# An inference step with 32 experts on one core: decode rows given eight places of their own in every expert tile, the prompt routed before the last cache pages, expert rows written straight to their tokens

## The chip, the core and the metric

The kernel runs on one core of one Trainium2 chip. The metric is device time in microseconds (us) of one execution, the median of several. Lower is better.

## What is computed

One layer of a decoder for 1024 prompt rows and 8 decode rows, width 1024, all in fp32:

```python
hn = rmsnorm(x, ln1_g);  q, k, v, u = split(hn @ w_in)
attn = diff_attend(rope(q), rope(k), v)       # prompt: causal, 1024 rows
                                              # decode: 64 cache pages of K and V per row
s5   = s5_mix(u, state)                       # diagonal state space group, GLU
x = x + concat(attn, s5) @ w_out
t = rmsnorm(x, ln2_g)
g = argmax(t @ w_rg + b_rg);  e1, e2 = top_2(t @ w_re[g] + b_re[g])   # 4 groups of 8 experts
x = x + sum_c wts[c] * ((silu(t @ w_gate[e_c]) * (t @ w_up[e_c])) @ w_down[e_c])
y = rmsnorm(x, ln_f_g)
```

The decode rows read the paged cache: 8 x 64 pages, each 256 KB of K and 256 KB of V.

## The kernel before, in words

**One list for TensorE.** `make_plan` (L170) is a list scheduler: from `streams` (L77), which gives each unit of work a cost and what it comes after, it makes one order in which TensorE does the units, and the other engines walk the same list. A page unit `("K", ...)` or `("V", ...)` covers eight pages. When it is placed is set by three numbers, `PAGE_US` (the time of a unit's transfer), `PAGE_LAG` (from the release of a place to its transfer) and `PACE` (the least distance of two page units). Engines run in order: a unit whose input is late holds up all behind it. `banks` deals six PSUM banks out to the units in the same order.

**Pages.** SyncE loads eight pages at a time (L476) into one half of `ring`, two halves in turn; the transfer into a half is issued when TensorE has used the half's last eight (`s_pgfree`). There are 128 page units in four passes of 32: K and V for decode rows 0 to 3, then K and V for rows 4 to 7. Between a K pass and its V pass stand `m1`, `m2`, `m3` and `pt`, the softmax over all scores; a V unit needs its result. After each row's V pages come `ov` (L1165) and, after the last, `dout` and `dout2` (L1173 to L1184): the norm of the decode attention, with a root on GpSimd (`root`, L538).

**Around the pages.** The prompt's projections, attention heads (`S`, `C`, `T`, `O`), the S5 group (`bA` to `bG`) and the output projection (`out`, unit halves of four 128x512 matmuls) fill TensorE between page units. Each row tile then passes `hn`, `hs`, `hT`, `r`: second norm, store to `h2_scratch` (L650), eight transposes (L1967), router logits. The decode rows are tile 8 (`NT`) of the same chain.

**Routing.** `choose` and `route` are appended after the whole plan. For all nine tiles at once VectorE picks group and experts (L1468 to L1516), TensorE ranks the choices within each expert (`rank`, matmuls of 320 columns and less), VectorE works out tile and place of each choice (L1526 to L1571), and TensorE makes the list of row numbers (`ids`). Each expert has a tile of 128 places; an expert with more rows gets another, out of at most 16 extra tiles. `s_route` then releases all engines.

**Experts.** A loop over tiles, four in each turn. GpSimd gathers a tile's rows from `h2_scratch` (L662, indirect), TensorE turns them (`turn`, L2014), VectorE scales (`scale`, L1608), then gate and up product (8 matmuls), tanh on ScalarE (L912), silu on VectorE (L1615, L1617), `turn_he` (L2028), the down product. ScalarE copies the result out (L923) and stores the tile's 128 rows in one direct transfer to `y_scratch` (L925). SyncE loads 3 MB of weights for each tile (L492, L493) into four places.

**The end.** When all is stored (`s_stored`), GpSimd gathers the two expert rows of every token (L685, 18 indirect transfers), VectorE adds them with their weights (L1640) and scales (L1653). A tile that may not have been written must read as zero or finite: GpSimd therefore writes 16 tiles of zeros to `y_scratch` during the u projection (L564).

## Time and profile before

| | us |
|---|---|
| median of 3 runs | 1621.96 (1618.86 to 1623.68) |
| profiled execution | 1610.36 |
| its span, first to last instruction | 1608.2 |
| TensorE busy | 1311.4 (82%) |
| VectorE busy | 515.3 (32%) |
| ScalarE busy | 250.8 (16%) |
| GpSimd busy | 203.2 (13%) |
| mean granted TensorE clock | 0.905 |
| moved by DMA | 467.51 MB, mean 291 GB/s |

The profiled execution is 11.6 us (0.7%) faster than the median of the others; its own outside part is 1610.36 - 1608.2 = 2.2 us. Busy shares are means over stages of different kinds. In the rows below a time is from the span's start, "PE" is TensorE, "PEld" its weight loads, "DVE" VectorE, "ACT" ScalarE, "POOL" GpSimd, "SPq" and "ACTq" the queues of SyncE and ScalarE. TensorE's rows count two instructions for each fp32 matmul of the program.

### The profile page before, as it was taken

How to read it: one execution, taken by the hardware profiler on the slowest of the kernel's cores; microseconds unless marked ns; L12 is line 12 of the kernel's file. 1: busy time of each engine (PE TensorE's matmuls, PEld its weight loads, DVE VectorE, ACT ScalarE, POOL GpSimd, SP SyncE). 2: the span in 40 equal slices, each digit the busy share in tenths (PEclk: the TensorE clock that was granted, in tenths of full speed). 3: DMA queues.
4: the chain of work that ended last, by engine and by line, in shares of the span. 5: the costliest groups of instructions: out<-in, count | busy, mean ns of one | idle time of the engine just before them, and what ended most of it. 6: DMA issues, size and time to landing. Idle time of an engine off the chain costs nothing.

```text
span 1608.2 us, 22029 instructions
## 1 busy us (share of the span) xinstructions
PE 1311.4 (82%) x6908; PEld 640.2 (40%) x6908; DVE 515.3 (32%) x1331; ACT 250.8 (16%) x472; POOL 203.2 (13%) x329
## 2 busy tenths in 40 slices
PE   4887998999879687688977698997359999999960
PEld 2333454443334234344543233444324444444420
DVE  1440343433243454344553011122501111111118
ACT  2100111121002222222342000000001111111112
POOL 1110304040310200000000100010011011010015
PEclk9898999998779799899987799998569999999985
DMA  9599999868878989899948999934239999999937
GB/s 360 205 351 348 315 326 310 294 182 311 252 236 296 313 302 321 291 337 329 347 166 286 379 336 318 320 99 161 107 144 334 369 366 369 367 371 366 365 114 271
DMA packets 187745, 467.51 MB, mean 291 GB/s; under 512 B 23177, under 2 KB 23561, under 8 KB 179090
## 3 DMA queue, kind: packets, MB, share of 16 engines
q1 hardware_dynamic: 163602, 386.02, 68.1%
q0 software_dynamic: 19456, 63.66, 11.1%
q10 hardware_dynamic: 4608, 16.78, 2.5%
q8 instruction: 50, 0.82, 0.2%
q14 instruction: 29, 0.24, 0.0%
HBM read 422.97 MB, written 42.22 MB: 289 GB/s over the span
## 4 chain that ended last, share of the span: by engine, by line
PE 60%; DMA 16%; SPq 9%; DVE 7%; issue 5%; DVEq 2%; ACT 1%; POOL 0%; ACTq 0%; POOLq 0%; PEldq 0%
PE WA L1671 42%; PE SC L1671 10%; DMA ring<-in_cacheV 8%; SPq L476 7%; DMA ring<-in_cacheK 7%; PE OD L1671 4%; PE WA L2014 2%; SPq L465 1%; DVE st L1084 1%; DVE arena L1640 1%; PE WA L1772 1%; DMA xm<-in_xT 1%; DVE arena L1653 1%; PE WA L1967 1%; DVEq L1642 0%
## 5 line engine op out<-in xcount | busy, mean ns | idle before, releaser
L1671 PE MATMUL WA<-arena,xm 128*128 128x512 f32 (+2 forms) x1024 | 423.0, 601 | 1.6 <-DVE xm L1608 1.4
L1671 PE MATMUL WA<-arena 128*128 128x128 f32 (+9 forms) x1188 | 239.7, 394 | 29.3 <-DVEq L1571 16.9
L1671 PEld LDWEIGHTS WA<-arena,xm 128*128 128x128 f32 (+1 forms) x1024 | 169.6, 181 | 215.0 <-issue 212.9
L1671 PE MATMUL SC<-ring,sall 128*32 128x512 f32 x1024 | 145.0, 692 | 73.2 <-DMA ring<-in_cacheV 51.5
L1671 PEld LDWEIGHTS WA<-arena 128*128 128x128 f32 (+2 forms) x1188 | 148.3, 200 | 118.5 <-issue 88.1
L1615 DVE SCALAR_TENSOR_TENSOR arena<-arena,WA 128x256 f32<-128x256 f32 x32 | 13.5, 421 | 298.1 <-ACT arena L912 298.1
L1671 PEld LDWEIGHTS SC<-ring,sall 128*32 128x32 f32 x1024 | 29.2, 118 | 157.7 <-issue 67.2
L1671 PE MATMUL WA<-xm,arena 128*128 128x512 f32 x192 | 90.8, 619 | 0.6 <-PE SC L1671 0.4
L1671 PE MATMUL SC<-ring,qpad 128*32 128x256 f32 x1024 | 69.8, 419 | 24.7 <-DMA ring<-in_cacheK 24.6
L538 POOL TENSOR_TENSOR st<-st,consts 128x1 f32<-128x1 f32 (+1 forms) x17 | 13.1, 770 | 562.3 <-DVEq L1118 393.7
L1671 PE MATMUL OD<-ring,qpad 128*32 128x256 f32 x1024 | 66.1, 402 | 20.1 <-DMA ring<-in_cacheK 20.1
L789 ACT ACTIVATE arena<-WA,st 128x128 f32<-128x128 f32 (+7 forms) x64 | 47.4, 740 | 148.4 <-DVEq L1088 148.4
L1671 PEld LDWEIGHTS SC<-ring,qpad 128*32 128x32 f32 x1024 | 32.2, 117 | 65.2 <-DMA ring<-in_cacheK 35.2
L1671 PE MATMUL WA<-xm 128*128 128x512 f32 x128 | 56.3, 593 | 0.8 <-DVE xm L1608 0.8
L1671 PE MATMUL WA<-ring,xm 128*128 128x512 f32 x128 | 56.3, 592 | 0.0
L1671 PEld LDWEIGHTS WA<-xm,arena 128*128 128x128 f32 x192 | 36.1, 198 | 44.5 <-issue 44.5
L1671 PEld LDWEIGHTS OD<-ring,qpad 128*32 128x32 f32 x1024 | 31.2, 114 | 56.5 <-DMA ring<-in_cacheK 28.4
L923 ACT ACTIVATE arena<-WA 128x1024 f32<-128x1024 f32 x32 | 32.8, 1024 | 125.8 <-PE WA L1671 125.8
L1671 PE MATMUL WA<-arena,consts 128*128 128x512 f32 (+10 forms) x68 | 26.3, 537 | 31.1 <-ACT arena L717 22.3
L1084 DVE TENSOR_REDUCE st<-WA 128x1 f32<-128x128 f32 (+7 forms) x64 | 48.5, 758 | 4.7
L2014 PE MATMUL WA<-consts,ring 128*128 128x128 f32 x256 | 34.1, 277 | 17.7 <-DMA ring<-h_scratch,idc 17.7
L912 ACT ACTIVATE arena<-WA 128x256 f32<-128x256 f32 x32 | 12.3, 383 | 222.2 <-PE WA L1671 222.2
(334 smaller groups left out, 1200.4 us busy)
## 6 DMA issues: line engine op xcount, KB each, us to landing
ring<-in_cacheK SPq DMA_DIRECT2D x512, 256.0 KB, 4.6
ring<-in_cacheV SPq DMA_DIRECT2D x512, 256.0 KB, 4.5
arena<-in_w_gu SPq DMA_DIRECT2D x16, 2048.0 KB, 10.9
arena<-in_w_dn SPq DMA_DIRECT2D x16, 1024.0 KB, 13.6
xm<-in_w_gu SPq DMA_DIRECT2D x8, 2048.0 KB, 11.5
ring<-in_w_gu SPq DMA_DIRECT2D x8, 2048.0 KB, 11.2
y_scratch<-arena ACTq DMA_DIRECT2D x32, 512.0 KB, 11.1
arena<-in_w_in SPq DMA_DIRECT2D x32, 256.0 KB, 9.9
```

The costliest lines, as they stand in the source:

```text
L465: sp.dma_start(w[:, k, :], io["w_in"][n, k, :, :]).then_inc(s_wk[k], 16)
L476: sp.dma_start(ring[:, GRP * half + j, :], cache[bass.ds(page, 1), :, :] .rearrange("a p n -> p (a n)")).then_inc(s_pg[half], 16)
L789: act.activation(P[:, n % 2, c, 0:w], slot("S", i, h, c)[:, 0:w], ACT.Exp, bias=st[:, 4 * (n % 2) + c:4 * (n % 2) + c + 1], scale=HD ** -0 ...
L923: act.activation(yb[v % 2], W[1][:, :], ACT.Copy).then_inc(m_ys, 1)
L1084: dve.reduce_max(st[:, 8 + c:9 + c], S[:, 0:w], AX)
L1615: dve.scalar_tensor_tensor(he[v % 2], tg[v % 2], 1.0, gu[:, 0:DE], ADD, MUL)
L1640: dve.scalar_tensor_tensor(x1[0:r, i, :], yg[i][c][0:r, :], wts[0:r, c, i:i + 1], x1[0:r, i, :], MUL, ADD)
L1653: dve.scalar_tensor_tensor(x1[0:r, i, :], x1[0:r, i, :], st[0:r, i:i + 1], lnf[0:r, :], MUL, MUL)\
L1671: return pe.matmul(out, lhsT, rhs, start=first, stop=last, **kw)
L1772: last = pe.transpose(slot("AT", i, h)[:, 128 * j:128 * j + 128], P[:, n % 2, 0, 128 * j:128 * j + 128], ident)
L1967: last = pe.transpose(slot("hT", i)[:, 128 * k:128 * k + r], h2[0:r, i % 2, 128 * k:128 * k + 128], ident[0:r, 0:r])
L2014: last = pe.transpose(W[0][:, 128 * k:128 * k + 128], hg[v % 2][:, 128 * k:128 * k + 128], ident)
```

## The change

- An expert tile has 120 places for prompt rows (`CAP`) and 8 for the decode rows, which every expert now computes; of its 8 decode results a row later reads the two it chose. 52 tiles at most.
- Choice and ranks take the eight prompt tiles only, as units of the plan (`pick1`, `pick2`, `rank`, `rt0`, `rt1`, `ids`, `lists`, `turn0`). Their places in the order are before the last V units. The decode rows' output projection, norm and logits stand behind the last V unit; their choice is made by VectorE inside the first four expert tiles (`pick_a`, `pick_b`, `pick_rows`, `pick_w`).
- A tile's 120 rows are scattered by GpSimd (indirect) to the rows of their tokens in `y_scratch`, and its 8 decode rows are stored by ScalarE to `y_dec`. The prompt's 16 reads at the end are direct transfers of SyncE; only the two of the decode rows stay indirect. Places without a token write to rows that nobody reads. The zero tiles are gone.
- Weight places are renamed: the first tile's weights load after the routing, the second's after the last page, the third's and fourth's after the decode rows' output projection.
- `scale` runs one tile further ahead of `silu`. The decode norm's sum goes into 32 partitions of one column, its root is one column wide, and a second small matmul spreads it.
- The planner's page numbers change.

```diff
-MAXT = 48
+CAP = 128 - NB
+MAXT = 52
-PAGE_US, PAGE_LAG, PACE = 5.75, 2.0, 6.4
+PAGE_US, PAGE_LAG, PACE = 6.0, 3.6, 7.1
@@ streams
-    dec += [(("dout",), 0.1, [(("ov", NB - 1), 2.0)]), (("dout2",), 0.0, [(("dout",), 7.0)])]
+    dec += [(("dout",), 0.1, [(("ov", NB - 1), 1.0)]), (("dout2",), 0.2, [(("dout",), 2.0)]),
+            (("out", NT), 4.0, [(("dout2",), 1.0), (("out", NT - 1, 1, 1), 0.0)]), (("hn", NT), 0.0, [(("out", NT), 2.0)]),
...
+    fin += [(("pick1",), 0.0, [(("r", NT - 1), 0.5)]), (("pick2",), 0.0, [(("pick1",), 5.0)]),
+            (("rank",), 0.9, [(("pick2",), 5.0)]), (("rt0",), 0.0, [(("rank",), 0.5)]), (("rt1",), 0.0, [(("rt0",), 9.0)]),
+            (("ids",), 2.0, [(("rt1",), 9.5)]), (("lists",), 0.0, [(("ids",), 0.5)]), (("turn0",), 1.0, [(("lists",), 9.0)])]
@@ make_plan
-    plan += [("choose",), ("route",)]
@@ sync
-            sp.wait_ge(*filled("o", NT))
-            weights(slice(0, 1), 0)
-            weights(slice(1, 2), 1)
-            sp.wait_ge(s_pgfree, RING // GRP + NB * 2 * NPAGE // GRP)
-            weights(slice(2, 3), 2)
-            sp.wait_ge(s_route, 1)
+            sp.wait_ge(s_route, 1)
+            weights(slice(0, 1), 0)
+            sp.wait_ge(s_pgfree, RING // GRP + NB * 2 * NPAGE // GRP)
+            weights(slice(1, 2), 1)
+            sp.wait_ge(*filled("o", NT))
+            weights(slice(2, 3), 2)
             weights(slice(3, 4), 3)
...
+            sp.wait_ge(s_stored, 1)
+            for i in range(NT):
+                for c in range(2):
+                    sp.dma_start(yg[i][c], io["y_scratch"][SEQ * c + 128 * i:SEQ * c + 128 * i + 128, :]).then_inc(f_g[i], 16)
@@ gpsimd
-                    for t in range(NE + 4 * n, NE + 4 * n + 4):
-                        gp.dma_start(io["y_scratch"][128 * t:128 * t + 128, :], zero_row).then_inc(s_zst, 16)
+            def scatter(q, v):
+                gp.wait_ge(m_ys, 4 * q + (v + 1))
+                gp.tensor_copy(idc[:, 2 + v % 2:3 + v % 2], dst[:, bass.ds(4 * q + v, 1)])
+                gp.drain()
+                gp.indirect_dma_start(io["y_scratch"], bass.IndirectOffsetOnAxis(ap=idc[0:CAP, 2 + v % 2:3 + v % 2], axis=0),
+                                      yb[v % 2][0:CAP, :], None).then_inc(m_st[v % 2], 16)
+            def lists():
+                gp.wait_ge(s_route, 1)
...
+                gather(0, 0)
...
+            with gp.Fori(0, n3) as q:
+                for v in range(4):
+                    gp.wait_ge(m_T, 4 * q + (v + 3))
+                    gather(q + 1, v)
+                    scatter(q, v)
@@ scalar, store
-                act.dma_start(io["y_scratch"][bass.ds(512 * q + 128 * v, 128), :], yb[v % 2]).then_inc(m_st[v % 2], 16)
+                act.dma_start(io["y_dec"][bass.ds(4 * NB * q + NB * v, NB), :], yb[v % 2][CAP:128, :]).then_inc(m_sd[v % 2], 16)
@@ vector
-            scale(0, 0)
+            scale(0, 1)
             for v in range(4):
                 silu(0, v)
-                scale(0, v + 1)
+                scale(0, v + 2)
+                if v == 0:
+                    pick_a(NT, T9)
...
@@ tensor, experts
-            turn(0, 0, first=True)
+            pe.wait_ge(s_h2T, NT + 1)
+            settled(4)
             gate_up(0, 0)
+            settled(0, 1, 5)
             turn(0, 1)
```

**TensorE from the last page unit on.** The list of before from the last V unit (the 8 matmuls from `ring,sall`), its first twelve rows; `arena,xm` are halves of the output projection, L1967 a tile's transposes, `wr` its logits, `wmap,o4s` the last `ov`, `aD,consts` `dout`:

```order
L1671 MATMUL SC<-ring,sall 32x512 x8
L1671 MATMUL SC<-dv,ptn 32x512
L1967 MATMUL WA<-consts,arena 128x128 x8
L1671 MATMUL WA<-arena,xm 128x512 x4
L1671 MATMUL OD<-wmap,o4s 128x1 x4
L1671 MATMUL WA<-wr,arena 128x36 x8
L1671 MATMUL WA<-arena,xm 128x512 x4
L1671 MATMUL WA<-aD,consts 128x32
L1671 MATMUL WA<-arena,xm 128x512 x12
L1967 MATMUL WA<-consts,arena 128x128 x8
L1671 MATMUL WA<-arena,xm 128x512 x4
L1671 MATMUL WA<-wr,arena 128x36 x8
```

The change's list from `ids` (128x52) through the last V unit to the first expert tile; `qpad` now holds the first gathered tile, L2095 turns it:

```order
L1754 MATMUL WA<-arena 128x52 x16
L1754 MATMUL SC<-ring,sall 32x512 x8
L1754 MATMUL SC<-dv,ptn 32x512
L1754 MATMUL OD<-wmap,o4s 128x1 x4
L1754 MATMUL WA<-consts,aD 32x1
L2095 MATMUL WA<-consts,qpad 128x120 x8
L1754 MATMUL WA<-rt,consts 128x32
L1754 MATMUL WA<-arena,xm 8x256 x32
L2055 MATMUL WA<-consts,arena 128x8 x8
L1754 MATMUL WA<-wr,arena 8x36 x8
L2155 TENSOR_LOAD plan_t
L2155 ISA x2
```

Before, 40 matmuls of the prompt's output projection, four tiles' transposes and logits, ranks and `ids` follow the last page unit; now only the decode rows' own work and the first tile's turn do.

**GpSimd at the first gather.** Before, from the store of a prompt tile to the first gather (`aD` is the decode norm's root, `st` a row tile's):

```order
L538 TENSOR_TENSOR aD<-aD,consts 128x32
L538 TENSOR_TENSOR st<-st,consts 128x1
L650 DMA h_scratch<-arena 128x1024
L538 TENSOR_TENSOR st<-st,consts 128x1
L650 DMA h_scratch<-arena 128x1024
L538 TENSOR_TENSOR st<-st,consts 128x1
L650 DMA h_scratch<-arena 8x1024
L670 DMA arena<-in_ln_f_g 128x1024
L660 COPY idc<-ids 128x1
L662 DMA ring<-h_scratch,idc 128x1024
```

Now:

```order
L653 DMA h_scratch<-arena 128x1024
L656 COPY idc<-ids 128x1
L658 DMA qpad<-h_scratch,idc 120x1024
L544 TENSOR_TENSOR st<-st,consts 32x1
L544 TENSOR_TENSOR st<-st,consts 128x1
L656 COPY idc<-ids 128x1
L658 DMA ring<-h_scratch,idc 120x1024
L686 DMA arena<-in_ln_f_g 128x1024
```

The first gather stands ahead of both roots of the decode rows.

**TensorE between the first K pass and its V pass.** Before (L1826 is `m2`, L1837 `pt`):

```order
L1745 MATMUL WA<-consts,arena 128x128 x4
L1671 MATMUL WA<-arena,xm 128x512 x4
L1826 MATMUL OD<-consts,mrow 1x128
L1671 MATMUL WA<-arena,xm 128x512 x4
L1671 MATMUL OD<-consts,mrep 128x1
L1671 MATMUL WA<-arena 128x136 x12
L1671 MATMUL WA<-arena,xm 128x512 x8
L1837 MATMUL WA<-consts,sall 128x128 x16
L1841 MATMUL WA<-consts,snew 8x128
L1671 MATMUL OD<-mrow,consts 128x1
L1671 MATMUL WA<-arena,xm 128x512 x4
L1671 MATMUL SC<-ring,sall 32x512 x16
```

Now:

```order
L1754 MATMUL WA<-arena,xm 128x512 x4
L1909 MATMUL OD<-consts,mrow 1x128
L1968 MATMUL WA<-consts,arena 128x128 x8
L1754 MATMUL OD<-consts,rt 128x1
L1754 MATMUL WA<-arena,xm 128x512 x4
L1920 MATMUL WA<-consts,sall 128x128 x16
L1924 MATMUL WA<-consts,snew 8x128
L1754 MATMUL OD<-mrow,consts 128x1
L1754 MATMUL WA<-arena,xm 128x512 x4
L1754 MATMUL SC<-ring,sall 32x512 x16
```

In this piece 20 projection matmuls and 12 of the S5 group have become 12 and 8 transposes.

## Rows read from the trace of the kernel before

**Rows 1.** Busy time by stretch: stretch, length, engines' busy us, PE clock, DMA share, GB/s.

```profile
68.50:1060.70 992.20, 832.40 (x5324) 396.13 (x5324) 356.23 (x997) 164.93 (x333) 114.58 (x205) 0.91 0.88 302
68.50:307.70 239.20, 205.11 (x1501) 97.66 (x1500) 90.72 (x317) 25.31 (x43) 45.66 (x84) 0.96 0.96 331
307.70:340.00 32.30, 31.86 (x154) 18.86 (x150) 12.39 (x24) 9.95 (x17) 7.45 (x15) 0.95 0.42 138
1060.70:1185.80 125.10, 71.34 (x345) 46.66 (x341) 42.23 (x120) 4.84 (x9) 13.06 (x15) 0.73 0.31 124
1185.80:1557.20 371.40, 367.06 (x1080) 177.95 (x1080) 62.08 (x95) 57.28 (x96) 34.13 (x59) 0.99 0.87 324
1557.20:1608.20 51.00, 0.00 (x0) 0.00 (x0) 35.33 (x36) 10.35 (x18) 29.18 (x27) 0.52 0.72 259
1320.00:1440.00 120.00, 120.00 (x357) 58.41 (x356) 21.17 (x32) 19.31 (x32) 12.54 (x22) 1.00 0.98 370
```

**Rows 2.** Waits of TensorE up to the last page: us in total, times, longest.

```profile
PE SC L1671 <- DMA ring<-in_cacheV: 51.5, 16, 10.7
PE SC L1671 <- DMA ring<-in_cacheK: 24.6, 12, 6.0
...
PE OD L1671 <- DMA ring<-in_cacheK: 20.1, 9, 5.8
```

**Rows 3.** Timeline of TensorE, last page to experts: start, us, what, idle before.

```profile
1060.65 1.04 PE L1671 MATMUL SC<-dv,ptn 8*32 8x512 f32 x2
...
1073.79 10.55 PE L1671 MATMUL WA<-arena,xm 128*128 128x512 f32 x24
...
1106.68 3.64 PE L1671 MATMUL WA<-arena,xm 128*8 128x256 f32 x64
...
1133.62 6.25 PE L1671 MATMUL WA<-arena,consts 128*128 128x320 f32 x20 [8.76 <-DVEq L1506]
1156.81 7.92 PE L1671 MATMUL WA<-arena 128*128 128x48 f32 x36 [16.95 <-DVEq L1571]
1182.41 1.97 PE L2014 MATMUL WA<-consts,ring 128*128 128x128 f32 x8 [17.68 <-DMA ring<-h_scratch,idc]
...
1185.79 9.40 PE L1671 MATMUL WA<-arena,xm 128*128 128x512 f32 x16 [1.41 <-DVE xm L1608]
```

**Rows 4.** Timeline of the other engines there.

```profile
1074.31 5.44 POOL L538 TENSOR_TENSOR aD<-aD,consts 128x32 f32<-128x32 f32 x1 [24.32 <-DVEq L1177]
...
1120.86 0.56 POOL L538 TENSOR_TENSOR st<-st,consts 128x1 f32<-128x1 f32 x1 [5.98 <-DVEq L1413]
...
1178.22 1.05 POOL L662 DMA_INDIRECT ring<-h_scratch,idc  x1 [12.05 <-issue]
...
1110.46 1.70 DVE L1405 TENSOR_TENSOR arena<-arena,WA 8x256 f32<-8x256 f32 x4 [3.47 <-PE WA L1671]
...
1112.31 1.05 ACT L893 ACTIVATE arena<-arena 8x1024 f32<-8x1024 f32 x1 [5.17 <-DVEq L1408]
...
1123.33 0.23 DVE L1426 TENSOR_TENSOR arena<-WA,colw 128x64 f32<-128x64 f32 x1 [1.14 <-PE WA L1967]
```

**Rows 5.** Timeline of a steady expert tile, TensorE and VectorE.

```profile
1375.73 1.04 PE L2014 MATMUL WA<-consts,ring 128*128 128x128 f32 x8
...
1377.18 1.22 DVE L1608 TENSOR_TENSOR xm<-WA,colw 128x1024 f32<-128x1024 f32 x1
...
1380.04 0.38 PE L2028 MATMUL SC<-consts,arena 128*128 128x128 f32 x2
```

**Rows 6.** DMA queues: packets, MB, share of 16 engines' span.

```profile
q0 software_dynamic: 19456, 63.66, 11.1%
q10 hardware_dynamic: 4608, 16.78, 2.5%
```

**Rows 7.** Timeline of the end: last store, first use of gathered rows.

```profile
1557.33 0.34 ACTq L925 DMA_DIRECT2D y_scratch<-arena  x1
...
1566.60 2.65 DVE L1640 SCALAR_TENSOR_TENSOR arena<-arena,wts 128x1024 f32<-128x1024 f32 x2 [18.38 <-DMA arena<-y_scratch,rows]
```

More of the change, by code:

```diff
@@ L72, in psum_keys @@
         "hT": [(("hT",) + a, 2)], "r": [(("r",) + a, 1)],
-        "dout": [(("dss",), 1)], "route": [(("rank",), 1), (("ids",), 1)],
+        "dout": [(("dss",), 1)], "dout2": [(("drep",), 1)], "rank": [(("rank",), 1)], "ids": [(("ids",), 1)],
+        "turn0": [(("t0",), 2)],
     }.get(k, [])
@@ L544, in dout @@
             def dout():
-                root(aD2[:, :, :].rearrange("p h b -> p (h b)"), ("dout",))
+                root(st[0:32, 30:31], ("dout",))
             def dqkv():
@@ new lines, in pick_rows @@
+            def pick_rows():
+                for c in range(2):
+                    dve.tensor_tensor(big8, OH8[c], consts[:, C_I32:C_I32 + NE], MUL)
+                    dve.drain()
+                    dve.reduce_sum(f9[:, NT:T9], big8, AX)
+                    dve.drain()
+                    dve.scalar_tensor_tensor(rows[:, c:c + 1], f9[0:NB, NT:T9], float(NB), consts[0:NB, C_TOK:C_TOK + 1], MUL, ADD)
+                    dve.drain()
+                dve.drain().then_inc(s_lst, 1)
+            r8t, q8t, e8t, b8t, g8t = (x[:, 0:NT] for x in (f9, gtop, gsum, t1, t2))
@@ L1998, in route, with turn @@
                 last.then_inc(full_sem("ids"), 1)
+            def turn(q, v, out=None):
+                pe.wait_ge(m_hg[v % 2], 32 * q + 16 * (v // 2 + 1))
+                if out is None:
+                    pe.wait_ge(m_hT, 4 * q + v)
+                for k in range(KD):
+                    last = pe.transpose((W[0] if out is None else out)[:, 128 * k:128 * k + CAP],
+                                        hg[v % 2][0:CAP, 128 * k:128 * k + 128], ident[0:CAP, 0:CAP])
+                last.then_inc(m_T, 1)
@@ L2000, in _, with turn0, settled @@
+            def turn0():
+                vacant(pe, "t0")
+                turn(0, 0, slot("t0"))
+                pe.wait_ge(m_T, 1)
+                pe.nop().then_inc(full_sem("t0"), 1)
+            def settled(*places):
+                for p in places:
+                    if USES[p]:
+                        pe.wait_ge(ps_free[p], USES[p])
             todo = {"stats": stats, "dqkv": dqkv, "dprep": dprep, "u": u, "k": k_, "kt": kt, "v": v, "q": q, "qt": qt,
                     "S": S, "T": T, "O": O, "ot": ot, "K": K, "m1": m1, "m2": m2, "m3": m3, "V": Vv, "pt": pt, "ov": ov,
-                    "dout": dout, "bP": bP, "bK": bK, "bX": bX, "bY": bY, "glu": glu, "out": out_, "hT": hT, "r": r_,
@@ L2003, in _ @@
-                    "route": route}
+                    "dout": dout, "dout2": dout2, "bP": bP, "bK": bK, "bX": bX, "bY": bY, "glu": glu, "out": out_, "hT": hT,
+                    "r": r_, "rank": rank_, "ids": ids_, "turn0": turn0}
             for unit in PLAN:
@@ L2006, in _ @@
                     todo[unit[0]](*unit[1:])
-            def turn(q, v, first=False):
-                pe.wait_ge(m_hg[v % 2], 32 * q + 16 * (v // 2 + 1))
-                if not (first and v == 0):
-                    pe.wait_ge(m_hT, 4 * q + v)
-                for k in range(KD):
-                    last = pe.transpose(W[0][:, 128 * k:128 * k + 128], hg[v % 2][:, 128 * k:128 * k + 128], ident)
-                last.then_inc(m_T, 1)
             def gate_up(q, v):
@@ L2047, in step @@
                     turn(q, v + 2)
+                if first and v == 0:
+                    settled(2, 3)
                 down(q, v, first)
```

367 lines of the change are left out of this document (207 added, 160 removed).

## The prediction

> **What bounds the kernel now.** I read the busy times by stretch first, then TensorE's waits, then the timeline around the last page, a steady expert tile, the DMA queues and the end. Four stretches follow each other.
>
> The page stretch runs from 68.5 to 1060.7 us. TensorE is busy 832.4 of its 992.2 us, so 159.8 us are idle [rows 1]. Page loads account for 51.5 + 24.6 + 20.1 = 96.2 us of TensorE's waits, 37 of them, at most 10.7 us each [rows 2]: TensorE works in order, and a page unit that stands too early holds up work that is ready. DMA is not the bound over the whole: the stretch moves 302 GB/s, while its first pass moves 331 at a share of 0.96 [rows 1]. The 302 x 992.2 = 299.6 MB would take 905 us at that rate.
>
> From the last page to the first expert product, 1060.65 to 1185.79 us, pass 125.1 us, with TensorE busy 71.3 of them [rows 1, 3] and page loads over. This holds the rest of the prompt's output projection, then a serial chain: ranks, VectorE's work, the list `ids`, the first gather.
>
> The experts are TensorE's: 371.4 us for 32 tiles, 11.6 each, 367.1 busy [rows 1]. DMA stands close behind: 370 GB/s at a share of 0.98 in the middle [rows 1].
>
> The end takes 51 us, from the last store at 1557.33; VectorE first works at 1566.60 [rows 1, 7].
>
> **Part 1, after the last page.** What leaves this stretch is the prompt's output projection, four tiles' transposes and logits, `rank`, `ids` and all between. What stays is the decode rows' chain, and perhaps the first gather.
>
> The decode chain: `ov`, `dout`, its root and `dout2` are small. In before's root 32 columns took GpSimd 5.44 us; one column takes 0.56 [rows 4]. I give these steps 6 us with their hops. The output projection of tile 8 is 3.64 us at the full clock [rows 3]; TensorE has been waiting often by then, and before it was granted 0.73 of its clock in this stretch [rows 1], so I take 5.5 us, between 3.64 and its double. Its addition starts at 1110.46 and the square ends about 1113.4; from the norm's root at 1120.86 to the scaled transposes 2.7 us pass (1123.33 + 0.23) [rows 4]. With hops that is 7 us. Sum 18.5 us.
>
> The gather chain can be later. GpSimd's first indirect transfer starts 12.05 us after it could [rows 4]; TensorE waited 17.68 us in all from the end of `ids` for the gathered tile, whose turn takes 1.97 [rows 3]. Nothing indirect runs earlier in the change, so I keep that price. The order has `ids`, one V unit, `ov`, `dout`, `turn0`, `dout2`: the turn stands ahead of the spread of the decode norm, and the first gather ahead of both decode roots on GpSimd. So `dout2` comes at 17.68 + 1.97, about 20 us after `ids`. Then come the projection and the 7 us: the first product starts 33 us after `ids`. The last page unit ends some 4 us after `ids` (between 2, if its pages have landed, and 7, if not). Last page to first product is then 29 us; the ends are 18.5, if the 12.05 does not come back, and 35. Saved: 125.1 - 29 = **96 us**.
>
> **Part 2, the page stretch takes in what left.** It receives 40 matmuls of the projection (10.55 us for 12 [rows 3], so 35.2), four tiles of transposes and logits at some 3 us, and `rank` and `ids`, 6.25 + 7.92 at the half clock [rows 3], so 7.1 at the full one: 54.6 us of TensorE's time. It gives back:
>
> - Page waits. Units now stand further apart in the order, so other work stands before a page not yet landed. With 96.2 us of such waits, 54.6 us of new work could at best vanish in them. I take 40: late in the stretch, TensorE has little but pages and VectorE's routing, and there waits stay.
> - The gap from the first K pass to its V pass. DMA falls to 138 GB/s for 32.3 us in which TensorE is busy 31.86 [rows 1]. The order takes 8 projection matmuls and 12 of S5 out and 4 transposes more in; at 0.88 us a matmul some 10 us less. They come back later as cover, so I count the 10 us.
> - The zero tiles: 16 x 0.52 = 8.4 MB in the first pass, the one where DMA has a share of 0.96: 25 us of transfer. TensorE has 205.1 of 239.2 us there [rows 1] and now gets more to do, so I count nothing.
>
> The last page then ends at 1060.65 + 54.6 - 40 - 10 = **1065 us**. From below: 832.4 + 54.6 us of work with no idle would end it at 955.5, and DMA at 331 GB/s, with 291 MB, at 948. From above: nothing gained back, 1115. I stay near the upper half because nothing here shows TensorE more than 0.86 busy over a pass [rows 1].
>
> The first product starts at 1065 + 29 = 1094, 92 us earlier.
>
> **Part 3, the experts.** Still 32 tiles: counting the reference's router over the prompt gives at most 90 rows to an expert. The turn is 120 columns of 128 wide; 1.04 us [rows 5] becomes some 0.06 less, 2 us over all tiles. In steady state VectorE scales before it does silu: the turn ends at 1375.73 + 1.04 = 1376.77, scaling (1.22) and silu (about 1 us) end near 1379.1, and `turn_he` comes at 1380.04 [rows 5]: covered by under 1 us. In the first four tiles VectorE's choice for the decode rows, some 10 small operations each, stands between and breaks that cover: +5 us once. On GpSimd gather and scatter cost some 2 us each of 11.6. The scatter moves half a MB per tile from q10 to q0. Per MB q10 took 2.5 / 16.78 = 0.149% of the span and q0 11.1 / 63.66 = 0.174% [rows 6]; for 16.3 MB that adds 0.4% of 1608, 6.6 us of all engines, over 32 tiles 0.2 us each, at a share of 0.98 [rows 1]. I take +1. Sum +4.
>
> **Part 4, the end.** The last result passes a small copy, a drain and an indirect issue of 1.05 us where a direct issue took 0.34 [rows 4, 7]: some +2. The first reads are direct and no longer queue one by one on GpSimd: -1. VectorE's nine tiles, 41.6 us from 1566.60 to the span's end [rows 7], stay as they are and bound the rest. Sum +1.
>
> What a page says of this step stands by itself: the Trainium skill (DMA: Bandwidth & Descriptors, "Anatomy of one DMA") fits a GpSimd transfer as 2.0 us and its bytes at 436 GB/s, an estimate of 3.1 us for the last scatter; the end would be about 1.5 longer by it. No run here shows an indirect store.
>
> **Sum.** -92 + 4 + 1 = -87 us. The profiled execution of 1610.36 becomes 1523; the median stands 11.6 above it, so 1621.96 - 87 = **1535 us**.
>
> **Rivals.**
>
> *The pages run closer than I grant.* All page waits but 20 us go, and the other idle stays. Then 54.6 - 76 - 10 ends the last page at 1029, 36 us before mine: 1499. For it: 96.2 us is a lot [rows 2]. Against: VectorE's waits and the in-order queue stay. 0.17.
>
> *Experts bound by DMA.* If a scattered row costs DMA twice a stored one, half a MB more per tile is 1.4 us at 370 GB/s, less 0.2 us of slack, 1.2 x 32 = 38 us: 1573. For it: the share of 0.98 [rows 1]. Against: the gathers, also one row of 4 KB at a time, fit beside the rest today. 0.12.
>
> The skill's page named above, in the section on why a DMA increments its semaphore by 16, lets a transfer run on the largest number of engines, up to 16, that divides its partitions. By that rule, 120 rows go to 15 engines with 32 KB each, as 128 rows do to 16, and the shorter tile saves the transfer nothing. No row of before has 120 partitions.
>
> *The route ends late.* `rank` and `ids` stand in TensorE's order with few pages between; if what stands between them (before, 8.76 + 6.25 + 16.95 + 7.92 = 39.9 us from the last logits to the list [rows 3]) outlasts the page units that stand there, pages wait behind them and the last page slips 30 to 45 us: 1572. 0.08.
>
> *Slower.* TensorE's order is worse filled, not better: each unit moved in among pages holds up the next load, which is issued only when a half is free. The stretch keeps its 159.8 us idle and adds 54.6 of work and over 36 of new idle, and the last page ends beyond 1065 + 87 = 1152. It decides at 887 of 1083.5 us busy, a share under 0.82; now it is 0.84 [rows 1]. With 0.81, the page ends at 1163 and the time is 1633. Against: the first-pass gap gets shorter, and the page numbers come nearer to what the trace shows. 0.04.
>
> **How the numbers follow.** Forecast 0.57, rivals 0.17, 0.12, 0.08, 0.04, nothing gained 0.02. The forecast's own bounds: last page 1045 to 1085, the next step 22 to 35, experts 0 to +15: 1508 to 1560. The range takes in the fast rival and the two middle ones: 1497 to 1575. A measurement here tells 0.3%, 5 us, from no change. Faster 0.94, the same 0.02, slower 0.04.
>
> **What would show it.** Right: last V unit near 1065; TensorE's waits for pages near 56 us; first product within 35 us of the last page and the 12 us gap on GpSimd before it; 11.4 us per steady tile; first combination 9 to 11 us after the last copy. Wrong: pages ending beyond 1115; tiles of 12 us or more; waits of `rank` or `ids` above 10 us; `turn_he` waiting for silu in steady state.

## The result and the profile after

| | before | changed |
|---|---|---|
| median of the runs, us | 1620.41 (1613.84 to 1623.68, 4 runs) | 1667.14 (1656.28 to 1677.19, 4 runs) |
| profiled execution, us | 1610.36 | 1661.91 |
| its span, us | 1608.2 | 1660.1 |

The ratio is 1.0289, 95% interval 1.0253 to 1.0325: the change made the kernel slower. I had forecast 1535. All profiles below are of executions within 1% of their kernel's median but one: that of the kernel with one drain for gather and scatter together took 1567.15 us against a median of 1548.35, and only the order of its instructions and the gaps between them are read from it.

The first view is the busy time by stretch of the changed kernel, in the columns of [rows 1]: pages, last page to first expert product, experts, end, and a piece of the steady loop.

```profile
68.50:1076.80 1008.30, 881.65 (x5522) 429.57 (x5518) 391.87 (x1101) 168.09 (x339) 111.44 (x198) 0.93 0.86 291
68.50:307.70 239.20, 227.27 (x1570) 110.90 (x1567) 101.87 (x333) 30.22 (x51) 43.22 (x79) 0.99 0.91 302
1076.80:1111.50 34.70, 11.29 (x109) 6.92 (x109) 6.12 (x18) 1.15 (x2) 4.26 (x7) 0.63 0.68 249
1111.50:1609.00 497.50, 402.61 (x1080) 194.42 (x1080) 65.42 (x129) 57.47 (x97) 74.94 (x123) 0.89 0.74 250
1609.00:1660.00 51.00, 0.00 (x0) 0.00 (x0) 35.32 (x36) 10.35 (x18) 6.68 (x11) 0.50 0.67 259
```

TensorE's waits up to the last page, which answer to [rows 2]:

```profile
PE SC L1754 <- DMA ring<-in_cacheV: 26.2, 9, 7.8
...
PE OD L1754 <- DMA ring<-in_cacheK: 17.0, 6, 5.9
```

With a third group of 7.6 us (K pages before `SC`) they are 50.8 us, where they were 96.2. TensorE's timeline from the last page unit to the first expert product answers to [rows 3]:

```profile
1075.78 1.04 PE L1754 MATMUL SC<-dv,ptn 8*32 8x512 f32 x2
...
1093.54 1.83 PE L2095 MATMUL WA<-consts,qpad 120*128 120x120 f32 x8 [13.86 <-DMA qpad<-h_scratch,idc]
...
1098.67 5.61 PE L1754 MATMUL WA<-arena,xm 128*8 128x256 f32 x64 [1.02 <-DVEq L1207]
...
1111.50 3.75 PE L1754 MATMUL WA<-arena 128*128 128x512 f32 x4
```

The front went the way that I had said, though not as far. The last page unit ends at 1075.78 (before: 1060.65), the first product comes at 1111.50 (before: 1185.79), 74.3 us sooner where I had 92. All the loss lies behind it: the experts take 497.5 us where they took 371.4 [rows 1]. The waits there, first TensorE's, then GpSimd's, from the first product on:

```profile
PE WA L2095 <- DMA qpad<-h_scratch,idc: 42.9, 8, 6.3
PE WA L2095 <- DMA ring<-h_scratch,idc: 41.8, 10, 6.1
PE SC L2130 <- DVE arena L1692: 3.0, 2, 2.1
```

```profile
POOL y_scratch L666 <- issue: 246.8, 32, 12.0
POOL qpad L658 <- issue: 84.9, 15, 16.2
POOL ring L658 <- issue: 72.3, 14, 8.5
```

L658 is the indirect gather, L666 the new indirect scatter. Between the copy of an index column and the transfer that reads it stands only a drain, and "issue" means that nothing the profile shows is waited for. These gaps sum to 404 us. GpSimd's timeline in a steady tile shows their pattern:

```profile
1388.36 1.00 POOL L658 DMA_INDIRECT ring<-h_scratch,idc  x1 [3.76 <-issue]
1389.36 0.19 POOL L664 COPY idc<-dst 128x1 uint32 x1
1401.18 1.03 POOL L666 DMA_INDIRECT y_scratch<-arena,idc  x1 [11.62 <-issue]
1402.21 0.20 POOL L656 COPY idc<-ids 128x1 uint32 x1
1406.21 1.00 POOL L658 DMA_INDIRECT qpad<-h_scratch,idc  x1 [3.80 <-issue]
```

And TensorE's, over the same tile (a turn, the first product, the next turn):

```profile
1382.55 1.86 PE L2095 MATMUL WA<-consts,qpad 120*128 120x120 f32 x8 [6.26 <-DMA qpad<-h_scratch,idc]
1384.21 4.51 PE L1754 MATMUL WA<-arena 128*128 128x512 f32 x8
...
1400.36 1.86 PE L2095 MATMUL WA<-consts,ring 120*128 120x120 f32 x8 [4.56 <-DMA ring<-h_scratch,idc]
```

The landings of the two transfers issued in this stretch, the gather of 1388.36 and the scatter of 1401.18, in us from issue (the list of DMA issues, for a window around each):

```profile
ring<-h_scratch,idc POOLq DMA_INDIRECT x1, 12.0
...
y_scratch<-arena,idc POOLq DMA_INDIRECT x1, 4.2
```

The gather issued at 1388.36 lands about 1400.3 and is waited for by the turn at 1400.36. The scatter whose column was copied at 1389.36 goes out at 1401.18, 0.86 us after that landing. That scatter lands about 1405.4, and the next gather goes out at 1406.21, 0.83 us after it. It is so for all: from the third gather on, 60 indirect transfers in a row are issued 0.82 to 0.90 us after the transfer before them has landed. GpSimd thus goes through gather and scatter one after the other, each from issue to landing. The tile shown takes 17.8 us from turn to turn (1382.55 to 1400.36); from the turn at 1123.23 to the thirtieth behind it at 1584.83 they take 15.4 on average, where a tile of [rows 5] takes 11.4.

TensorE pays twice. It waits 84.7 us for gathered rows, ahead of 18 of its turns, and it is busy 402.6 us for the same 1080 instructions that took 367.1: the granted clock of the stretch is 0.89 where it was 0.99, and after a wait the turn takes 1.86 us and the first eight product rows 4.51, against 1.04 in [rows 5] and 3.60 at the full clock. 84.7 + 35.5 + some 5 of `silu` waits is the stretch's 126 us.

### The profile page after: what moved, and what is told of

Same layout as the page of the kernel before. It is cut to its first block, busy times and chain, and to the rows that moved or that the text cites. A ratio compares the mean times of both kernels' runs of the same rounds, so it can differ in the third digit from the quotient of the medians.

```text
span 1660.1 us, 22275 instructions
## 1 busy us (share of the span) xinstructions
PE 1336.5 (81%) x6904; PEld 650.6 (39%) x6904; DVE 518.0 (31%) x1369; ACT 251.1 (15%) x473; POOL 207.6 (13%) x359
## 3 DMA queue, kind: packets, MB, share of 16 engines
q0 software_dynamic: 19424, 61.53, 11.7%
## 4 chain that ended last, share of the span: by engine, by line
PE 42%; issue 30%; DMA 9%; DVE 7%; SPq 4%; POOLq 4%; DVEq 2%; ACT 1%; POOL 1%; ACTq 0%; PEldq 0%
PE WA L1754 28%; PE SC L1754 9%; DMA ring<-in_cacheK 4%; PE OD L1754 4%; SPq L480 3%; DMA ring<-in_cacheV 2%; POOLq L657 2%; POOLq L665 2%; SPq L469 1%; DMA ring<-h_scratch,idc 1%; DVE st L1102 1%; PE WA L1855 1%; DVE arena L1723 1%; DMA xm<-in_xT 1%; DVE arena L1118 1%
## 5 line engine op out<-in xcount | busy, mean ns | idle before, releaser
L1754 PE MATMUL WA<-arena 128*128 128x512 f32 (+10 forms) x1440 | 363.5, 437 | 24.5 <-issue 14.4
L1754 PE MATMUL WA<-arena,xm 128*128 128x512 f32 (+2 forms) x768 | 312.0, 611 | 8.1 <-DMA arena<-in_w_out 5.9
L1754 PEld LDWEIGHTS WA<-arena 128*128 128x128 f32 (+2 forms) x1440 | 198.1, 199 | 171.0 <-issue 151.8
L1754 PEld LDWEIGHTS WA<-arena,xm 128*128 128x128 f32 (+1 forms) x768 | 122.1, 180 | 163.1 <-issue 155.1
L1669 DVE TENSOR_TENSOR arena<-WA,colw 128x960 f32<-128x960 f32 x16 | 18.5, 1158 | 214.4 <-PE WA L2095 214.4
L1669 DVE TENSOR_TENSOR xm<-WA,colw 128x960 f32<-128x960 f32 x16 | 18.5, 1157 | 207.9 <-PE WA L2095 176.3
L544 POOL TENSOR_TENSOR st<-st,consts 128x1 f32<-128x1 f32 (+2 forms) x18 | 13.8, 767 | 517.2 <-DVEq L1136 314.7
L2095 PE MATMUL WA<-consts,qpad 120*128 120x120 f32 x128 | 22.8, 340 | 56.7 <-DMA qpad<-h_scratch,idc 56.7
L666 POOL DMA_INDIRECT y_scratch<-arena,idc x32 | 32.8, 1025 | 246.8 <-issue 246.8
L2095 PE MATMUL WA<-consts,ring 120*128 120x120 f32 x128 | 22.9, 341 | 41.8 <-DMA ring<-h_scratch,idc 41.8
## 6 DMA issues: line engine op xcount, KB each, us to landing
arena<-in_w_dn SPq DMA_DIRECT2D x16, 1024.0 KB, 11.6
```

Of the source, the lines that this page charges most:

```text
L666: gp.indirect_dma_start(io["y_scratch"], bass.IndirectOffsetOnAxis(ap=idc[0:CAP, 2 + v % 2:3 + v % 2], axis=0), yb[v % 2][0:CAP, :], None) ...
L1669: dve.tensor_tensor(hgT[v % 2][:, :, 0:CAP], (W[0] if src is None else src)[:, :] .rearrange("p (k n) -> p k n", k=KD)[:, :, 0:CAP], colw[ ...
L1754: return pe.matmul(out, lhsT, rhs, start=first, stop=last, **kw)
L2095: last = pe.transpose((W[0] if out is None else out)[:, 128 * k:128 * k + CAP], hg[v % 2][0:CAP, 128 * k:128 * k + 128], ident[0:CAP, 0:CAP])
```

## The experiments

**Theory D**: the drain on GpSimd does not end before the indirect transfers that GpSimd has issued have landed. Then gather and scatter in one loop, with a drain ahead of each, serialize. **Rival Q**: the transfers themselves hold each other up, in their queue or because scattered rows are dear, and the drain only shows it. Beside them stand smaller questions, on the page numbers (theory P), on the place of the first turn (theory T) and on the zero tiles. Times are medians; ratios are against runs of the kernel before on the same chip, whose median was 1618.45 for `a_nodrain`, `b_drain2`, `b_nodrain` and `a_nd_w1`, 1621.49 for `a_pair`, `a_nd_turn`, `a_nd_oldpace` and `b_newpace`, and 1621.93 for the other four. Where runs of different groups are compared, the ratios are the safer measure.

### The changed kernel without drains

The copy raises a semaphore, GpSimd waits for that, and a nop takes the place of the drain. Nothing else changes, and the order of copy and transfer stays safe.

```diff
-                gp.tensor_copy(idc[:, v % 2:v % 2 + 1], ids[:, bass.ds(4 * q + v, 1)])
-                gp.drain()
+                gp.tensor_copy(idc[:, v % 2:v % 2 + 1], ids[:, bass.ds(4 * q + v, 1)]).then_inc(s_ic, 1)
+                gp.wait_ge(s_ic, 2 * n)
+                gp.nop().then_inc(s_ic, 1)
...
-                gp.drain()
+                gp.wait_ge(s_ic, 2 * n)
+                gp.nop().then_inc(s_ic, 1)
```

> The change, with the drain between the copy of a tile's row numbers and the indirect transfer replaced by a wait on the copy's own semaphore, for gathers and scatters. Theory D (a GpSimd drain also waits until the indirect transfers already in flight have landed, so gather and scatter of a tile run one after the other, 15.0 us a tile): the gaps of 5 to 12 us before the scatters go to about 1 us, a steady tile takes 11.4 us, and the time falls by about 32 x 3.6 = 115 us to 1552. Theory Q (the queue of indirect transfers itself does not take a second one while one is in flight): the gaps stay, whatever the instruction before, and the time stays at 1667. Theory M (scattered 4 KB rows are dear for DMA): the gaps go, but transfers land later, and a tile takes 13 us or more: above 1600.

Measured: 1545.79 us (1541.79 to 1551.6), ratio 0.9537 [0.9484, 0.959]. The steady loop of this kernel by GpSimd's timeline:

```profile
1386.87 0.18 POOL L657 COPY idc<-ids 128x1 uint32 x1 [4.79 <-PE WA L2098]
1387.90 1.01 POOL L660 DMA_INDIRECT qpad<-h_scratch,idc  x1 [0.85 <-POOLq L659]
1391.49 0.18 POOL L666 COPY idc<-dst 128x1 uint32 x1 [2.58 <-ACT arena L941]
1392.55 1.02 POOL L669 DMA_INDIRECT y_scratch<-arena,idc  x1 [0.87 <-POOLq L668]
```

and by TensorE's:

```profile
1385.71 0.99 PE L2098 MATMUL WA<-consts,qpad 120*128 120x120 f32 x8
1386.54 3.60 PE L1757 MATMUL WA<-arena 128*128 128x512 f32 x8
...
1397.07 0.98 PE L2098 MATMUL WA<-consts,ring 120*128 120x120 f32 x8
```

Every gap in this stretch is 0.85 to 0.87 us, a tile is 11.36 us, no turn of the steady loop waits. From 1380 to 1440 TensorE is busy all 60 us, while DMA moves 359 GB/s with the same scattered rows:

```profile
1380.00:1440.00 60.00, 60.00 (x179) 29.02 (x178) 9.54 (x15) 9.33 (x16) 13.16 (x22) 1.00 1.01 359
```

Scatters here take longer to land (median 13.3 us, gathers 13.0), and no turn waits for them. The same transfers without the drains: 121 us off the time. D holds, Q falls.

### The changed kernel, one drain for gather and scatter together

```diff
                     gp.wait_ge(m_T, 4 * q + (v + 3))
-                    gather(q + 1, v)
-                    scatter(q, v)
+                    gp.wait_ge(m_ys, 4 * q + (v + 1))
+                    gp.tensor_copy(idc[:, v % 2:v % 2 + 1], ids[:, bass.ds(4 * q + 4 + v, 1)])
+                    gp.tensor_copy(idc[:, 2 + v % 2:3 + v % 2], dst[:, bass.ds(4 * q + v, 1)])
+                    gp.drain()
+                    gp.indirect_dma_start(hg[v % 2][0:CAP, :], None, io["h2_scratch"],
...
+                    gp.indirect_dma_start(io["y_scratch"], bass.IndirectOffsetOnAxis(ap=idc[0:CAP, 2 + v % 2:3 + v % 2], axis=0),
```

> a_nodrain, with one drain in each tile of the expert loop put back: both copies, one drain, then gather and scatter one behind the other. Theory D: that drain waits for the pair before it to land, which is issued 11.4 us earlier and takes up to 18 us beside the weights; the wait is seen before each pair, and a tile takes 11.4 to 13 us, well under the 15.0 of the change: 1546 to 1595. Theory Q would hold both transfers apart: a gap of 4 us or more between the two indirect issues, and 15 us a tile.

Measured: 1548.35 us, ratio 0.9542 [0.9504, 0.958], the same as without drains. GpSimd's timeline in its loop:

```profile
1393.57 0.18 POOL L695 COPY idc<-ids 128x1 uint32 x1 [5.67 <-ACT arena L945]
1393.70 0.17 POOL L696 COPY idc<-dst 128x1 uint32 x1
1397.04 1.00 POOL L698 DMA_INDIRECT qpad<-h_scratch,idc  x1 [3.16 <-issue]
1398.34 1.01 POOL L701 DMA_INDIRECT y_scratch<-arena,idc  x1 [0.30 <-issue]
```

The two transfers follow each other in 0.30 us where no drain is between them, so the queue takes both. The one drain still costs 3.2 us in the tile shown and 4.3 on the average of the loop's 28, the rest of the landing of the pair before; that much fits beside TensorE. The gather here also goes out only when the tile's results are there, and even that late it is in time. A drain as such did no harm in this kernel; the harm was a drain just behind an issue.

### The kernel before, a second drain behind each gather of the loop

```diff
                     gather(q, v)
+                    gp.tensor_copy(idc[:, 2 + v % 2:3 + v % 2], ids[:, 0:1])
+                    gp.drain()
+                    gp.tensor_copy(idc[:, 2 + v % 2:3 + v % 2], ids[:, 0:1])
```

> The kernel before, with one more copy and drain, and a copy that marks its end, behind every gather of the expert loop; nothing waits for them. Theory D: the second copy starts only when the gather has landed, 4 to 9 us after its issue, and the time stays at 1620, since GpSimd has that much room in 11.4 us. Theories Q and M: the marking copy follows the first within 1.2 us.

Measured: 1620.39 us (1614.1 to 1630.41), ratio 1.0012 [0.9985, 1.004]. The row of L682 is the copy behind the drain:

```profile
1377.14 0.96 POOL L662 DMA_INDIRECT ring<-h_scratch,idc  x1 [0.76 <-issue]
1378.09 0.20 POOL L680 COPY idc<-ids 128x1 uint32<-128x1 uint32 x1
1387.96 0.18 POOL L682 COPY idc<-ids 128x1 uint32<-128x1 uint32 x1 [9.67 <-issue]
```

The same drain that costs some 0.8 us with nothing in flight takes 9.67 here, and 3.07 to 10.16 over the loop, 157 us in 28 of them. In each of the 28 the copy behind the drain starts 0.15 us after the gather has landed: 1377.14 + 10.7 is 1387.8 for the one shown. This ties the end of the drain to the landing, whatever is issued next. The time does not move, since GpSimd has nothing else to do in a tile of before. This is why its profile gave me no warning: every steady drain stood over 9.4 us behind the last issue, when the gather (median 6.1 us to landing) had landed.

### The kernel before without drains

The same edit of `gather` alone, in the kernel before.

> The kernel before, with the same replacement at its gathers. Theory D: the 12.05 us before its first indirect transfer were the drain waiting for the 512 KB load of the final norm's weights issued just ahead, and the 3.7 us before the second and third were the first and second gather; all fall below 1.5 us, the first product comes 8 to 12 us sooner, and the time is 1610 against 1620. Theory Q or a first-use cost: the 12 us stay or fall only in part, and the time does not move by more than 4 us.

Measured: 1621.38 us (1613.43 to 1628.82), ratio 1.0006 [0.9977, 1.0035]; a miss. The gap that I had counted at 12.05 us went:

```profile
1180.19 0.57 POOL L671 DMA_DIRECT2D arena<-in_ln_f_g  x1 [42.10 <-DVEq L1595]
...
1181.85 1.06 POOL L663 DMA_INDIRECT ring<-h_scratch,idc  x1 [0.89 <-POOLq L662]
```

So the gap belonged to the drain. Most of it was the wait for the `ln_f_g` load issued just ahead, which landed 9.8 us after its issue at 1165.40, about 1175.2. But the gather of before went out at 1178.22, 3.0 us behind that landing and not 0.8 as elsewhere: some 2 us of the 12.05 stay open. The gather, issued 11 us earlier relative to the load, then travels beside that load and the weights (11.4 us to landing, 4.1 before), and TensorE's turn still waited 13.74 us, where it was 17.68 [rows 3]: 4 of 11 came through. And the span's end lost as much: the last store is issued at 1616.86 of 1623.9 us, 7.0 before the end, against 1605.96 of 1608.2, 2.2, in the profile of before.

### The first turn and the weights

Two edits of the kernel without drains. In `a_nd_w1` the second expert's weights wait for the first turn; in `a_nd_turn` the first turn stands behind the decode rows' output projection.

```diff
             sp.wait_ge(s_pgfree, RING // GRP + NB * 2 * NPAGE // GRP)
+            sp.wait_ge(m_T, 1)
             weights(slice(1, 2), 1)
```

> a_nodrain, with the second tile's 3 MB of weights issued only after TensorE has turned the first gathered tile. In the change that gather took 11.4 us to land behind 6 MB of weights, and TensorE waited 13.9 us for it. If the weights ahead of it make the gather late (theory W): it lands within 9 us, and the first product comes 3 to 6 us sooner than in a_nodrain. If not: the same within 2 us.

Measured: 1550.62 us, ratio 0.9578 [0.9531, 0.9625]. The turn's wait fell from 6.54 to 5.27 us, the last page to the first product from 29.2 to 28.3, not the 3 to 6 us that I had given theory W; no gain in the time.

```diff
-... (("turn0",), 1.0, [(("lists",), 9.0)])]
+... (("turn0",), 1.0, [(("lists",), 9.0), (("out", NT), 0.0)])]
```

> a_nodrain, with the turn of the first gathered tile placed behind the decode rows' output projection in TensorE's order, not ahead of the spread of the decode norm. In a_nodrain 28.0 us passed from the last page unit to the first product, and TensorE waited 6.5 us for the gathered tile with the decode rows' chain behind it. Theory T (that place of the turn holds the decode chain up): the wait goes, and the step takes 20 us, so 8 us less: 1538. Rival (weights and gather share DMA, and the decode rows' chain is as long): the step takes 26 us or more.

Measured: 1536.03 us (1525.31 to 1541.76, 6 runs), ratio 0.9468 [0.9432, 0.9504]. TensorE's timeline in its profile:

```profile
1076.41 1.91 PE L1757 MATMUL SC<-dv,ptn 8*32 8x512 f32 x2
...
1084.79 5.15 PE L1757 MATMUL WA<-arena,xm 128*8 128x256 f32 x64 [0.94 <-DVEq L1210]
1089.87 1.04 PE L2098 MATMUL WA<-consts,qpad 120*128 120x120 f32 x8
...
1097.58 9.08 PE L1757 MATMUL WA<-arena 128*128 128x512 f32 x16
```

The turn no longer waits, and 21.2 us pass from the last page to the first product. The projection is done while the gather travels. This has the lowest median of all versions, though its interval overlaps that of `a_nodrain` a little and that of the next run by much. Both edits together:

> The changed kernel without drains, with the first turn behind the decode rows' output projection, and the second expert's weights issued after that turn. If the first gather's landing still holds the first tile there, it lands sooner and the time falls from 1536 to about 1532. If the first product already waits for the decode chain alone, the later weights give nothing: 1536 to 1541, as they cost 5 us with the turn in front.

Measured: 1539.11 us (1535.13 to 1542.6), ratio 0.9497 [0.9455, 0.9538]. 19.5 us from last page to first product, but later weights win nothing.

### The page numbers

```diff
-PAGE_US, PAGE_LAG, PACE = 6.0, 3.6, 7.1
+PAGE_US, PAGE_LAG, PACE = 5.75, 2.0, 6.4
```

First the old numbers in the changed kernel without drains, then the new ones in the kernel before:

> a_nodrain, with the page numbers of before (5.75, 2.0, 6.4). If the new numbers are what lets the page stretch take in the moved work (theory P): waits for pages rise from 53 us towards 96, the last page ends 30 to 40 us later than the 1081 of a_nodrain, time 1580. If the moved work itself fills the waits: the last page within 10 us of 1081 and the time at 1546.

> The kernel before, with the page numbers of the change (6.0, 3.6, 7.1) and nothing else. Theory P: waits for pages fall from 96 us to about 50, the last page ends 20 to 40 us earlier than 1061, and the time is 1590. Else: within 8 us of 1620, since prompt work that is left over then stands behind the last page.

Measured: 1606.23 us (1599.7 to 1606.46), ratio 0.9898 [0.986, 0.9936], and 1595.85 us (1592.37 to 1598.08), ratio 0.9839 [0.9803, 0.9875]. The new numbers give 26 us to the kernel before and some 60 to the changed one; the rest of the change, without drains and with the old numbers, gives 15. In the kernel before they do not work as I had expected: page waits fall to 66.5 us, not to 50, and the last page ends at 1087.0, 26 us later than before and not 20 to 40 sooner. What moves ahead of it is prompt work, and the first product comes 12 us sooner (1173.77) in these profiles. What the 60 are is in TensorE's timeline with the old numbers:

```profile
1054.51 1.04 PE L1757 MATMUL SC<-dv,ptn 8*32 8x512 f32 x2
...
1084.54 10.55 PE L1757 MATMUL WA<-arena,xm 128*128 128x512 f32 x24
...
1144.25 7.07 PE L1757 MATMUL WA<-arena 128*128 128x52 f32 x32 [16.37 <-DVEq L1630]
1165.89 1.84 PE L2098 MATMUL WA<-consts,qpad 120*128 120x120 f32 x8 [14.56 <-DMA qpad<-h_scratch,idc]
```

The pages end 25 us earlier, at 1054.51 instead of 1079.83, but the prompt's output projection, the ranks and the list are again behind them: the planner, taking pages for close, places them early and the prompt late. The first product comes at 1169.07, 60 us after that of the new numbers. The new lists of work only allow the prompt to be routed beside pages; the numbers make it happen. I had expected 1580 for this run, with longer waits and a last page 30 to 40 us later. The waits are longer, 84.4 us against 53.1, but the page comes sooner: the moved work is the larger part.

Last, the distance alone, in the version with the turn moved (7.1 there):

> As a_nd_turn, the planner's distance of page loads 6.8 us in place of 7.1 (which moves page units a little closer together). Theory P (page numbers that are too small let units stand ahead of their pages; 6.4 with the two others old cost 60 us): slower than 1536 by 5 to 20 us. Rival P2 (7.1 is already too wide, the last page comes later than it has to): faster by up to 10.

> As a_nd_turn, the distance 7.4 us in place of 7.1. Theory P with room left: 1526 to 1536, fewer waits for pages. Rival P2: the last page ends later by up to (7.4 - 7.1) x 128 half loads = 38 us by the plan, some of it real: 1540 to 1560.

Measured: 1544.83 us (ratio 0.9539 [0.948, 0.9597]) with 6.8 and 1574.51 us (0.9711 [0.9674, 0.9748]) with 7.4. The waits for pages are 46.1 us with 7.1 and 47.0 with 6.8, so the mechanism of theory P is not seen there: the last page unit ends at about 1084 in place of 1076 at equal waits, and the difference in time is not clear of noise, since the two intervals overlap. With 7.4 the last page unit ends only at about 1122: eight V units stand behind `ids` with hardly any work between them, and page waits grow to 55.5 us. P2 is shown on that side, by more than the 1540 to 1560 that I had given; that 7.1 is better than 6.8 is not shown.

### The zero tiles

The kernel before with each zero tile written twice, the second time to a scratch tensor that nobody reads.

```diff
                         gp.dma_start(io["y_scratch"][128 * t:128 * t + 128, :], zero_row).then_inc(s_zst, 16)
+                        gp.dma_start(io["z_scratch"][128 * (t - NE):128 * (t - NE) + 128, :], zero_row).then_inc(s_zst, 16)
...
-                    act.wait_ge(s_zst, 16 * (MAXT - NE))
+                    act.wait_ge(s_zst, 32 * (MAXT - NE))
```

> The kernel before, each of the 16 zero tiles written a second time, to rows of a scratch tensor that nothing reads, in the same place of GpSimd's queue (8.4 MB more in the first pass). Theory Z0 (what I counted in the prediction: the zero tiles are worth nothing, since TensorE has 205 of 239 us in that pass): within 5 us of before, 1621. Rival Z1 (the pass is bound by DMA, 8.4 MB at 331 GB/s): +25 us, 1646, with a longer first pass and more waits for K pages.

Measured: 1640.18 us (1638.97 to 1645.17), ratio 1.0113 [1.0076, 1.015]: 18 us, near the 25 of the transfer. TensorE's waits for pages up to the end of the last one:

```profile
PE SC L1672 <- DMA ring<-in_cacheV: 58.5, 16, 11.6
PE SC L1672 <- DMA ring<-in_cacheK: 41.3, 12, 10.9
...
PE OD L1672 <- DMA ring<-in_cacheK: 19.2, 12, 4.1
```

They are 119.0 us, 22.8 more than in [rows 2]. A doubled cost says what one more copy costs; that leaving one out gives as much is likely, since the first pass's share was 0.96 [rows 1] and is 0.91 after, but was not tried by itself.

## Why the prediction was wrong, and where it was right

**The step that failed** stands in Part 3: "On GpSimd gather and scatter cost some 2 us each of 11.6." I summed copies, drains and issues as if they were work, 4 us in a tile that has 11.6, and saw no limit. The drain is no work but a wait, and what it waits for is the landing of the transfer issued just ahead. In the trace it measured 246.8 us ahead of 32 scatters and 157.2 ahead of 29 gathers. The experts took 124 us more from first product to TensorE's last (1111.50 to 1605.65, before 1185.79 to 1556.11) in place of my 4. By profile the parts are -74.3 to the first product, +123.8 in the experts and +2.4 at the end, where I had -92, +4 and +1. The sign of the result hangs on the middle one alone: with the drains gone the same kernel gives 1545.8, which the range would have held, 11 us from the forecast, or -72.7 against my -87 as a change. My range gave the experts +15 at most, since I took GpSimd for free. Of my signs of being wrong this one came: tiles of 12 us or more. (My bounds, added up, give 1504 and 1572, not the 1508 and 1560 that I wrote; nothing hangs on it.) No rival of mine had GpSimd as the limit: "Slower", at 0.04, stood for a last page beyond 1152, and it came at 1075.8, so the slower kernel does not bear that rival out.

The rows that could have told me were among mine: the gap of 12.05 us at the first gather [rows 4], right behind the `ln_f_g` load. I named it as a price, carried it over, and did not ask what it was. GpSimd's timeline of before holds two more:

```profile
1179.28 0.20 POOL L660 COPY idc<-ids 128x1 uint32<-128x1 uint32 x1
1183.16 0.98 POOL L662 DMA_INDIRECT ring<-h_scratch,idc  x1 [3.68 <-issue]
1184.45 0.18 POOL L660 COPY idc<-ids 128x1 uint32<-128x1 uint32 x1 [0.32 <-PE WA L2014]
1188.30 0.96 POOL L662 DMA_INDIRECT ring<-h_scratch,idc  x1 [3.67 <-issue]
```

Three drains just behind an issue took 12.05, 3.68 and 3.67 us, and those behind a longer pause some 0.8. The second and third gather went out 0.8 us after the gather before them had landed. The pattern of D was in the profile of before.

**Part 1** said 29 us from last page to first product. Without drains it is 29.2 (1079.83 to 1109.01); in the change itself 35.7, as the turn at 1093.54 waited 13.86 us for a gather that a drain had held back 6.61 us. The order that I described, with the turn ahead of the decode norm's spread, was the one that ran; its cost, though, was avoidable, as `a_nd_turn` shows. That the 29 was met without drains is partly luck. I had carried the gap of 12.05 us over as a price of the first indirect transfer; the gap was 0.99 there, and the gather's own way took 11.1 us from issue to landing, beside two experts' weights, where it had been 4.1. The turn came 10.5 us after the last page unit (I had 13.7), and from the turn to the first product passed 18.6 us (I had some 15).

**Part 2** said 1065 us for the last page. It was 1075.8, and 1079.8 without drains. Page waits are 50.8 us against "near 56", so that term was right in size. What brought them down is the page numbers, though, not the moved work: with the old numbers and the work moved they are 84.4. The work of TensorE up to there grew by 881.65 - 832.40 = 49.3 us, against 54.6. Its idle time fell from 159.8 to 1008.30 - 881.65 = 126.7, by 33, where I had 50. The page waits gave 45 of it, but other waits grew by 12 where I had them fall by 10. Those 10 I now take to be counted twice: the gap between the first K and V pass did get shorter (the first V unit starts at 323.91 where it was 339.98, and DMA moved 254 GB/s from 307.7 to 340 in place of 138), but TensorE was busy there before too, so an earlier page can only show as a shorter page wait, and these I had already. The 12 are a balance of small waits, of the same view as above. The largest was 6.3 us before:

```profile
PE WA L1754 <- issue: 14.4, 7, 3.4
```

Two single waits are new, 5.9 us for `in_w_out` and 4.9 for VectorE, and some others shrank. All three rows are there in `b_newpace` too (12.5, 6.4 and 4.9 us), so they come with the page numbers.

That I counted nothing for the zero tiles was a second miss, hidden in the same sum: they are worth some 18 us by the doubled run, with TensorE busy 0.86 of that pass. A stage's average slack does not cover a load whose pages are waited for one by one.

The page numbers stood in my sum only as part of the order. They carry some 60 us of it, by the two runs without drains.

**Part 3, the rest.** Without drains, TensorE's experts take 1109.01 to 1487.09, 378.1 us: 7.8 more than before against my 4. The first tiles' waits for `silu`, 5.0 us, are the +5 that I gave VectorE's choice for the decode rows. Tiles are 11.36 us, as forecast, and the silu order is covered in steady state.

The rival of experts bound by DMA did not come: 359 GB/s at full TensorE. Without drains, queue 0 used 12.0% of the span for 61.53 MB, 3.02 us per MB; by [rows 6] it was 11.1% for 63.66, 2.80. The queue with the scattered rows in it took some 8% more per MB, not double; how much of that is the rows and how much the other traffic was not tried.

**Part 4** said +1. The first combination starts at 1617.35, 9.4 us after the last scatter was issued (1607.95), as before (9.3 from the last store to the first use, [rows 7]). The end counts 54.5 us behind TensorE's last product, where it was 52.1: +2.4. Without drains it is 59.5 (1546.6 - 1487.09), of which some 5 lie behind the last store, as the last section says.

The Trainium skill (DMA: Bandwidth & Descriptors, "Anatomy of one DMA") gives a fit from which I had estimated 3.1 us for a GpSimd transfer of this size. The traces differ: 4.2 us is the median of the scatters in the changed kernel, and 13.3 without drains, where DMA moves 359 GB/s in all. The measured landings decide.

## What to carry to other kernels

Read each drain on GpSimd as a wait for the transfers that GpSimd has issued (drains of the other engines were not tried), and ask what will be in flight when the change puts a second issue ahead of it. Order an index copy ahead of its indirect transfer with the copy's own semaphore, or gather all copies ahead of one drain and issue back to back. An unexplained gap in the profile of before that the change will multiply is the first thing to measure, not a price to carry over.

## What the runs showed of the hardware

- A GpSimd drain took 0.8 us with nothing of GpSimd's in flight, and up to 16.2 us with a transfer of its own in flight, by what was left of that transfer (3.16 in the tile of `a_pair`, the 9.67 of the marked drain in `b_drain2`, the 11.62 in the changed kernel, and 16.20 there behind its `ln_f_g` load). It ended with the landing: a copy behind it started 0.15 us after, 28 times of 28, and an indirect transfer was issued 0.82 to 0.90 us after, 60 times in a row. Two indirect issues without a drain between them stand 0.30 us apart.
- An indirect gather of 120 rows of 4 KB took 4.9 to 13.6 us from issue to landing in the changed kernel, and 13.0 at the median without drains. That longer way cost nothing there, as the next tile's gather is issued a tile ahead.
- Every kernel in which the drain was replaced by a semaphore wait and a nop ends later behind its last store's issue: 7.0 to 7.7 us (1616.86 of 1623.9, 1538.94 of 1546.6), against 2.2 to 2.6 in all kernels with drains (1657.67 of 1660.1, 1562.66 of 1565.3 with one drain per pair). The profile shows no instruction there. What it is stays open; it also means that up to the last store the drainless versions are some 5 us better than their times say.
- The first drain of the changed kernel, at 1074.23, cost 6.61 us though GpSimd had been idle for 54.59 us before the copy by the profile; with one drain per pair it was 6.62 there, and 0.99 with the semaphore. By the profile no transfer of GpSimd's was in flight, so D does not explain this one; it was not tried further. The 2 us that stay open in the 12.05 of before are at the first such drain too.
- Over the changed kernel's expert tiles TensorE idled up to 6.3 us ahead of 18 turns, and the granted clock fell to 0.89 over the stretch. The same 1080 instructions took 35.5 us longer. A wait in TensorE's loop costs its length and, here, four tenths of it again.
